# A hybrid conformer / latent-attention / MoE layer: the last reads start one pair earlier, and one-hot and diagonal products add up the last rows

## The reference

```python
for l in range(DEPTH):
    ...
    h = _modulate(xs, g_pre2[l], sh2, sc2)
    xs = xs + gt2 * _rmsnorm(_hier_moe(h, *moe_w), g_post2[l])

def _hier_moe(h, ...):            # 32 experts in 4 groups of 8
    ...                           # one group per token, then the best two experts in it
    e_w = e_top / jnp.sum(e_top, axis=-1, keepdims=True) * g_top
    gates = jnp.sum(jax.nn.one_hot(expert_id, N_EXPERTS) * e_w[..., None], axis=1)
    for e in range(N_EXPERTS):
        he = jax.nn.silu(xt @ w_gate[e]) * (xt @ w_up[e])
        out = out + gates[:, e:e + 1] * (he @ w_down[e])
```

## Time and profile before

| | us |
|---|---|
| median of 3 runs | 673.69 (672.23 to 675.0) |
| the profiled execution | 672.28 |
| its span in the trace | 670.4 |
| PE busy in the span | 575.3 (86%) |
| DVE, ACT, POOL busy | 258.6, 154.7, 54.2 |
| HBM traffic over the span | 269 GB/s |

### The profile page before, as it was taken

The page is one execution under the profiler, slowest core; times in us unless marked ns, Lnnn a source line. Parts: engine busy times, 40 slices in busy tenths (PEclk is TensorE's granted clock), DMA queues, the critical chain, the costliest instruction groups (busy, mean ns, idle before and its releaser), DMA issues.

```text
span 670.4 us, 9777 instructions
## 1 busy us (share of the span) xinstructions
PE 575.3 (86%) x3945; PEld 344.1 (51%) x3945; DVE 258.6 (39%) x470; ACT 154.7 (23%) x318; POOL 54.2 (8%) x77
## 2 busy tenths in 40 slices
PE   0899999999998999999999869988998999777810
PEld 0766665655755455554444756454555555444400
DVE  2414999999533434403333560110101111000017
ACT  3320000012215444422222431111112111111125
POOL 6000000100000000000000010111121121110001
PEclk9999999999899999999999989989999999999965
DMA  9999956000006370009211829999999999999969
GB/s 328 359 385 401 412 199 229 7 8 1 1 1 254 132 294 21 1 9 387 105 64 63 314 58 406 392 407 423 425 421 422 426 423 423 422 425 425 374 246 264
DMA packets 47288, 173.58 MB, mean 259 GB/s; under 512 B 5402, under 2 KB 11899, under 8 KB 34938
## 3 DMA queue, kind: packets, MB, share of 16 engines
q1 hardware_dynamic: 39856, 158.74, 59.2%
q0 software_dynamic: 6096, 12.47, 5.7%
q10 hardware_dynamic: 1274, 1.52, 0.6%
HBM read 162.98 MB, written 17.06 MB: 269 GB/s over the span
## 4 chain that ended last, share of the span: by engine, by line
PE 69%; DMA 14%; SPq 6%; DVE 4%; ACT 3%; issue 3%; ACTq 1%; DVEq 0%; POOLq 0%
PE ps L1496 13%; PE ps L1750 10%; PE ps L1883 10%; PE ps L1899 6%; DMA arena<-in_w_up 6%; SPq L507 5%; DMA arena<-in_w_down 5%; PE ps L1501 4%; PE ps L1497 4%; PE ps L1514 3%; PE ps L1560 3%; PE ps L1709 3%; PE ps L1742 3%; PE ps L1696 2%; DMA x<-in_x_sample 2%
## 5 line engine op out<-in xcount | busy, mean ns | idle before, releaser
L1883 PE MATMUL ps<-arena 128*64 128x256 f32 x992 | 112.4, 384 | 9.6 <-DMA arena<-in_w_gate 4.3
L1496 PE MATMUL ps<-arena 128*128 128x512 f32 x200 | 103.1, 597 | 0.7 <-issue 0.6
L1883 PEld LDWEIGHTS ps<-arena 128*64 128x64 f32 x992 | 72.7, 138 | 52.5 <-issue 13.9
L1150 DVE SCALAR_TENSOR_TENSOR arena<-arena 128x655 f32<-128x655 f32 x116 | 94.8, 897 | 0.4 <-issue 0.2
L1899 PE MATMUL ps<-arena 128*64 128x512 f32 x256 | 60.0, 611 | 16.0 <-ACT arena L992 12.8
L1750 PE MATMUL ps<-arena 128*128 128x512 f32 x160 | 69.7, 594 | 1.9 <-DVE arena L1270 1.0
L1501 PE MATMUL ps<-cst,arena 128*128 128x128 f32 (+2 forms) x349 | 52.0, 297 | 20.0 <-DVE arena L1089 17.0
L1497 PEld LDWEIGHTS ps<-arena 128*128 128x128 f32 x200 | 38.0, 190 | 47.8 <-issue 47.8
L1501 PEld LDWEIGHTS ps<-cst,arena 128*128 128x128 f32 (+2 forms) x349 | 44.6, 180 | 30.3 <-issue 26.9
L1439 DVE TENSOR_TENSOR arena<-arena,ps 128x256 f32<-128x256 f32 x16 | 6.7, 421 | 112.7 <-ACT arena L1021 112.7
L1750 PEld LDWEIGHTS ps<-arena 128*128 128x128 f32 x160 | 30.0, 190 | 38.1 <-issue 37.0
(11 more groups left out here) (272 smaller groups left out, 568.8 us busy)
## 6 DMA issues: line engine op xcount, KB each, us to landing
arena<-in_w_up SPq DMA_DIRECT2D x15, 2048.0 KB, 26.9
arena<-in_w_down SPq DMA_DIRECT2D x15, 2048.0 KB, 20.0
arena<-in_w_gate SPq DMA_DIRECT2D x14, 2048.0 KB, 17.1
arena<-in_w_ada SPq DMA_DIRECT2D x12, 2048.0 KB, 13.5
arena<-y_d SPq DMA_DIRECT2D x10, 512.0 KB, 7.0
arena<-in_w_out SPq DMA_DIRECT2D x1, 4096.0 KB, 13.7
arena<-ada_d SPq DMA_DIRECT2D x8, 512.0 KB, 8.2
x<-in_w_gate SPq DMA_DIRECT2D x2, 2048.0 KB, 27.8
```

Source lines behind the costliest of these rows:

```text
L1150: ins = dve.scalar_tensor_tensor(dst, src, w, dst, ALU.mult, ALU.add)
L1496: mm(pp(name)[:, 0:TS], lhs(k), rhs_s(k), start=k == 0, stop=k == steps - 1)
L1883: last = mm(ps[a:a + ROWS, s, n * FE:(n + 1) * FE], src[:, k, a:a + ROWS], w[:, j, k * FE:(k + 1) * FE], start=k == 0, stop=k == KD - 1)
```

## The change

1. **Zeros first.** Early on, after the first three weight loads, SP writes zeros over the whole of `y_d` (5.2 MB) and waits for that.
2. **The last pair stays in SBUF.** Pair 15 isn't scattered. Its 128 rows are added by a product with `last_hot`, a matrix of 128 rows by 640 tokens with the row's weight in its token's column. DVE makes it from a table of token numbers (`tokens`, a new transfer of 320 KB), the row's token and the row's weight. POOL fetches these weights: it writes `wsel` to HBM after pair 3 and gathers one value per row after pair 5.
3. **Reads earlier.** The ten reads of `y_d` wait for pair 14's scatter and no longer for pair 15; `x_again` is issued behind them.
4. **First shares on PE.** PE multiplies each block's first rows by a diagonal matrix of their weights, in float32 into PSUM, together with the last pair's rows: 4 products of 128x128 by 128x512 a block, and for blocks 3 and 4 two more for the second rows. For blocks 0 to 2 DVE adds the second rows. ACT's scaling goes.
5. **The last norm's vectors.** Instead of two transfers of 512 KB spread over the partitions, SP fetches one partition's row of 2048 values (8 KB). It is issued when pair 13's down product is done, behind the last weight load. PE spreads it by products with a row of ones: `last_gain(0)` ahead of pair 15's gate matmuls, `last_gain(1)` in place of the first `keep_busy`. ACT copies the results out of PSUM.
6. Some semaphores are joined under one name.

The diff, cut to its core:

```diff
+        nothing = W[:, KD * 2 * C + 4096:KD * 2 * C + 4096 + D]
+        tokens = arena[:, 2 * SLOT - 2048:2 * SLOT - 2048 + T]
+        last_hot = arena[:, 2 * SLOT - 2048 + T:2 * SLOT - 2048 + 2 * T]
+        diag0 = arena[:, 2 * SLOT - 2048 + 2 * T:2 * SLOT - 2048 + 3 * T]
...
+        gg2_row = x[0:1, 2:4, :].rearrange("p a b -> p (a b)")
+        last_token, last_weight = stat[:, 2, 0:1], stat[:, 4, 0:1]
+        ON_PE = NT - 2
...
+        LATE_BANK = (0, 2, 6, 4, 0)
+        def summed(b):
+            return ps[:, LATE_BANK[b]:LATE_BANK[b] + 2, :].rearrange("p a b -> p (a b)")
...
             landed(sp, "lnv")
             for n in range(3):
                 load(n)
+            sp.wait_ge(zeroed, 2)
+            sp.dma_start(y_d.rearrange("(n p) d -> p n d", p=P), nothing.unsqueeze(1).broadcast_to([P, 2 * NT, D])).then_inc(y_zero, 16)
+            sp.wait_ge(y_zero, 16)
...
+            sp.wait_ge(e_y, PAIRS - 2)
+            sp.wait_ge(ada_st[5], 32)
+            sp.dma_start(gg2_row, ada_flat[0:2, 5 * D:6 * D]).then_inc(gg2_in, 16)
             sp.wait_ge(e_y, PAIRS - 1)
-            sp.wait_ge(ada_st[5], 32)
-            for v in range(2):
-                sp.dma_start(gg2[:, v, :], bcast(v, 5)).then_inc(gg2_in, 16)
-            for b in range(ADDED, NT):
-                sp.dma_start(x_again[:, b - ADDED, :], out_rows(b)).then_inc(xa_in, 16)
-            for s in range(2):
-                sp.wait_ge(y_st[s], 16 * PAIRS // 2)
+            sp.dma_start(tokens, i["consts"][:, C_ALL:]).then_inc(tables_in, 16)
+            sp.wait_ge(y_st[0], 16 * PAIRS // 2)
+            sp.wait_ge(y_st[1], 16 * (PAIRS // 2 - 1))
             sp.wait_ge(r_pair, PAIRS)
-            sp.wait_ge(e_y, PAIRS)
             for b in range(NT):
                 for c in range(2):
                     sp.dma_start(yg[:, c, b, :], y_d[c * T + b * P:c * T + (b + 1) * P, :]).then_inc(yg_in[b], 16)
+            for b in range(ADDED, NT):
+                sp.dma_start(x_again[:, b - ADDED, :], out_rows(b)).then_inc(xa_in, 16)
             for b in range(ADDED, NT):
                 sp.wait_ge(f_norm, b + 1)
...
+            gp.wait_ge(y_zero, 16)
...
+                if pair == PAIRS - 1:
+                    return
                 gp.wait_ge(e_ys, pair + 1)
-                if pair == PAIRS - 1:
-                    gp.wait_ge(e_ysb, 1)
                 scatter(ys[:, s, :], ids[:, 0, pair:pair + 1], y_st[s])
+                if pair == 3:
+                    gp.wait_ge(wsel_ready, 1)
+                    gp.dma_start(w_d.rearrange("(p n) one -> p (n one)", p=P), wsel[:].rearrange("p c t -> p (c t)")).then_inc(row_weight, 16)
+                if pair == 5:
+                    gp.wait_ge(row_weight, 16)
+                    gp.indirect_dma_start(last_weight, None, w_d, bass.IndirectOffsetOnAxis(idx[:, 2:3], 0),
+                                          bounds_check=P * 2 * NT - 1, oob_is_err=False).then_inc(row_weight, 16)
...
+            def last_gain(v):
+                act.wait_ge(gg2_ps, v + 1)
+                act.activation(gg2[:, v, :], ps[:, 6:8, :].rearrange("p a b -> p (a b)"), ACT.Copy).then_inc(gg2_ready, 1)
...
             def expert_pair(pair, s, last=False, first=False):
                 n = act.value_load(extra[0:1, bass.ds(pair, 1)], min_val=0, max_val=ROUNDS - 1)
+                if last:
+                    last_gain(0)
                 act.wait_ge(e_gu, pair + 1)
                 act.activation(he[:, s, :], ps[:, s, 0:FE], ACT.Silu).then_inc(e_silu, 1)
...
             def norm_sum(b):
-                act.wait_ge(f_mix, b + 1)
-                act.activation(yjunk, yg[:, 1, b, :], ACT.Square, accum_out=stat[:, 3, b:b + 1]).then_inc(f_ss, 1)
+                if b < ON_PE:
+                    act.wait_ge(f_mix, b + 1)
+                else:
+                    act.wait_ge(f_more, b + 1)
+                act.activation(yjunk, yg[:, 1, b, :] if b < ON_PE else summed(b), ACT.Square, accum_out=stat[:, 3, b:b + 1]).then_inc(f_ss, 1)
                 act.wait_ge(f_ss, b + 1)
                 act.activation(stat[:, 5, b:b + 1], stat[:, 3, b:b + 1], ACT.Sqrt, bias=eps, scale=1.0 / D).then_inc(f_sd, 1)
...
             act.activation(stat[0:1, 6, 0:1], stat[0:1, 7, 0:1], ACT.Sqrt)
+            last_gain(1)
             act.wait_ge(e_y, PAIRS)
             act.wait_ge(y_st[1], 16 * (PAIRS // 2 - 1))
             act.activation(ys_last[:, 512:], ps[:, 5, :], ACT.Copy).then_inc(e_ysb, 1)
             for b in range(NT):
-                act.wait_ge(yg_in[b], 32)
-                act.activation(yg[:, 0, b, :], yg[:, 0, b, :], ACT.Copy, scale=wsel[:, 0, b:b + 1]).then_inc(f_first, 1)
-                if b:
-                    norm_sum(b - 1)
-            norm_sum(NT - 1)
+                norm_sum(b)
...
+            row, block = ids[:, 0, PAIRS - 1:PAIRS], idx[:, 3:4]
+            step(dve.tensor_scalar(block, row, P.bit_length() - 1, None, ALU.arith_shift_right))
+            step(dve.tensor_scalar(block, block, -float(P * 2 * NT - 1), None, ALU.mult))
+            dve.scalar_tensor_tensor(idx[:, 2:3], row, float(2 * NT), block, ALU.mult, ALU.add)
+            dve.tensor_copy(last_token, idg[:, 0, PAIRS - 1:PAIRS])
             dve.drain().then_inc(wsel_ready, 1)
...
+                if last:
+                    for b in range(NT):
+                        diag = dve.tensor_scalar(diag0[:, b * P:(b + 1) * P], ident, wsel[:, 0, b:b + 1], None, ALU.mult)
+                    diag.then_inc(hot_ready, 1)
+                    dve.wait_ge(tables_in, 112)
+                    dve.wait_ge(row_weight, 32)
+                    dve.tensor_scalar(last_hot, tokens, last_token, last_weight, ALU.is_equal, ALU.mult).then_inc(hot_ready, 1)
+                    dve.drain()
+                    for b in range(ON_PE, NT):
+                        diag = dve.tensor_scalar(diag1(b), ident, wsel[:, 1, b:b + 1], None, ALU.mult)
+                    diag.then_inc(hot_ready, 1)
...
-            dve.wait_ge(gg2_in, 32)
-            for b in range(NT + 1):
-                if b < NT:
-                    dve.wait_ge(f_first, b + 1)
-                    dve.scalar_tensor_tensor(yg[:, 1, b, :], yg[:, 1, b, :], wsel[:, 1, b:b + 1], yg[:, 0, b, :], ALU.mult, ALU.add)\
-                        .then_inc(f_mix, 1)
-                if b:
-                    n = b - 1
-                    dve.wait_ge(f_sd, n + 1)
-                    dve.reciprocal(stat[:, 5, n:n + 1], stat[:, 5, n:n + 1])
+            def mixed(b):
+                dve.wait_ge(f_more, b + 1)
+                dve.wait_ge(yg_in[b], 32)
+                dve.scalar_tensor_tensor(yg[:, 1, b, :], yg[:, 1, b, :], wsel[:, 1, b:b + 1], summed(b), ALU.mult, ALU.add).then_inc(f_mix, 1)
+            def normalised(b):
+                dve.wait_ge(f_sd, b + 1)
+                dve.reciprocal(stat[:, 5, b:b + 1], stat[:, 5, b:b + 1])
+                dve.drain()
+                src = yg[:, 1, b, :] if b < ON_PE else summed(b)
+                last = dve.scalar_tensor_tensor(yo[:, b, :], src, stat[:, 5, b:b + 1], gg2[:, min(b, 1), :], ALU.mult, ALU.mult)
+                if b >= ADDED:
                     dve.drain()
-                    last = dve.scalar_tensor_tensor(yo[:, n, :], yg[:, 1, n, :], stat[:, 5, n:n + 1], gg2[:, min(n, 1), :], ALU.mult, ALU.mult)
-                    if n >= ADDED:
-                        dve.drain()
-                        dve.wait_ge(xa_in, 16 * (NT - ADDED))
-                        last = dve.tensor_tensor(yo[:, n, :], yo[:, n, :], x_again[:, n - ADDED, :], ALU.add)
-                    last.then_inc(f_norm, 1)
+                    dve.wait_ge(xa_in, 16 * (NT - ADDED))
+                    last = dve.tensor_tensor(yo[:, b, :], yo[:, b, :], x_again[:, b - ADDED, :], ALU.add)
+                last.then_inc(f_norm, 1)
+            mixed(0)
+            dve.wait_ge(gg2_ready, 2)
+            for b in range(1, ON_PE):
+                mixed(b)
+                normalised(b - 1)
+            for b in range(ON_PE - 1, NT):
+                normalised(b)
...
+            def last_gain(v):
+                for half in range(2):
+                    at = v * D + half * 512
+                    one = mm(ps[:, 6 + half, :], ones[0:1, :], gg2_row[:, at:at + 512], start=True, stop=True)
+                one.then_inc(gg2_ps, 1)
...
+                if last:
+                    pe.wait_ge(gg2_in, 16)
+                    last_gain(0)
                 gate_up(s, first, xT[:, s], e_gate, e_gu, pair == 0)
                 if pair == 0:
...
+                if last:
+                    pe.wait_ge(gg2_ready, 1)
                 with pe.If(n > 0):
...
                 if last:
-                    keep_busy(3, 7)
+                    last_gain(1)
                 pe.wait_ge(e_h, pair + 1)
                 hidden_to_columns(s, he[:, s, :], e_ht)
                 if last:
-                    keep_busy(3, 7)
+                    keep_busy(3, 0)
                 pe.wait_ge(e_hT, pair + 1)
...
```

(63 more changed lines are left out.)

9 lines of the change are left out of this document (3 added, 6 removed).

## The result

The changed kernel is slower: 680.88 us median of 20 runs (676.37 to 686.66) against 674.92 of the kernel before (20 runs, 671.91 to 679.46), ratio 1.008 with a 95% interval of 1.0063 to 1.0098. The forecast was 672.9 in a range of 664 to 678, so the time lies outside the range, and it moved the other way than the likeliest case.

What follows compares the result with a forecast made beforehand. Weight loads set the experts' pace, then a serial tail. Row landing at 631.5, plus 16.2 to the down product's end, 14.3 for products and 7.7 finish: 669.7 against 670.4, so -0.7, 672.9 us; range 664 to 678.

Steps and rivals of the forecast that it cites:

- the likeliest case: Whole kernel: PE waits for the 8 KB row, and the time changes by -0.7 us to 672.9; chance 0.5.
- 24, at 0.597 = 14.3: PE's sums after the last down product: 24 products of 128x512 at 0.597 us each, 14.3 us.
- The saving in the tail: Stretch behind the last down product: shrinks from 31.3 to 22.0 us, a saving of 9.3.
- The row's queue: SP's DMA queue before pair 15: the 8 KB row waits behind the last weights, and PE waits for it until 631.5.
- G: Time the 8 KB row lands and PE can start on it: 631.5, the middle of 627.8 and 635.3.
- the slowest engine carries a part: Rival on the row's transfer: it lands at 635.3, making the kernel 3.1 to 4.1 us slower; chance 0.23.
- The terms behind the row: From the row's landing to pair 15's down product's end: `last_gain(0)`, gate and up, `last_gain(1)`, down product; 16.2 us.
- Gate and up: Pair 15's gate and up matmuls on PE after the row's wait: 8.7 us, with the clock lowered after the pause.
- The chances: Likeliest case 0.5, no wait for the row 0.2, slowest engine 0.23, reads late or something else 0.07.
- The covers: Early reads (9 us of cover), zeros, DVE's matrices and ACT's copies: hidden behind other work, taken to cost nothing.
- the finish behind the last product: Block 4, from its complete sum to the span's end: 7.7 us.

Runs made afterwards that it cites:

- the two kernels that repeat this stretch: Changed kernel with 20 products in the tail instead of 24, ratio 1.0071; changed kernel with the 8 KB row as two transfers, ratio 1.0087.

## Why the prediction was wrong

**The step that failed** is the term "24, at 0.597 = 14.3". A float32 product of 128x512 leaves two records in the trace, which overlap: each lasts 0.597 us, but in a long run a product takes 0.86 to 0.87. The "x200" of the earlier trace rows counts records, and the kernel there has half as many products. The stream took 20.87 us, 6.5 more than the sum had. The rows ahead of the prediction held the sign: each call of `keep_busy` makes three products and stands in the earlier trace rows as x6. The 64 and 16 matmuls that the description of the kernel before gives for a pair are such counts too; the code issues 32 and 8.

With that term alone set right the sum would have stood at +5.9 us instead of -0.7, where the ratio says +5.4. That it comes so near is partly luck, since two other errors nearly cancel (below). The saving in the tail, forecast as 9.3 us, was 3.0 (31.2 to 28.2). The one-hot half of the stream (10 products, 8.7 us) costs nearly what the scatter and the reads behind it had cost, 9.4.

**The row's queue** was right as a mechanism; the length of the wait wasn't. G was forecast as 631.5 in a trace in which pair 14's down product ended at 623.8, so a wait of 7.7 us. The row landed at 611.06 + 19.45 = 630.5, but everything ran 1.7 us later there, and PE waited 5.2 us, and 4.3 and 4.5 in the two kernels that repeat this stretch: 2.5 to 3.4 us less than forecast. Taking the middle of the engines' finishing times was a guess; the row's two engines were among the early ones. The queue explains the wait (it is gone on another queue), and the wait explains the loss against the kernel before (8 us come back without it, more than the 5.4 lost, and 6.6 us more of it cost about 7.5 us). What it doesn't explain is the distance from the forecast, which had a longer wait in it. The Trainium skill's rule on the share of the engines (DMA: Bandwidth & Descriptors, section Why a DMA increments its semaphore by 16 and not by 1), that only the engines which carry a transfer count, agrees with the trace: two landings for this row, sixteen for the one that was cut. The rival "the slowest engine carries a part" became true only then. Its wait was as forecast (635.3 - 623.8 = 11.5, measured 11.8). Its step above the main case, 7.5 us where 3.8 had been forecast, was larger mainly because the main case's own wait was shorter.

**The terms behind the row** were too small together: from PE's start on the row to the down product's end 18.7 to 21.8 us (in the four kernels that wait for it) where 16.2 had been forecast. In the changed kernel's trace, the 21.8, `last_gain(0)` took 3.75 instead of 1.2: the same miscount (0.87 a product) at half the clock; at full clock it is 1.98. Gate and up took 9.8 instead of 8.7 (8.5 to 9.5 in the other three). From there to the down product 3.3 instead of 2.6, since `last_gain(1)` has the miscount as well. The down product took 4.9 instead of 3.7, at the lower clock, which no step had foreseen and which is absent in the other three. The wait came out too long by 2.5 and these terms too short by 5.6, so that the last pair took 26.9 us where 23.9 had been forecast; in the two that repeat it, 23.0 and 23.5, the errors cancel. In this trace the misses of last pair and tail, 3.0 and 6.2 us, and the later end of pair 14 (1.7) make up the whole distance from 669.7 to 680.6.

**The chances** were misplaced for a reason of their own. The sum stood 0.7 us below zero with every unknown rounded the kind way: the slowed ones products were kept for the range's end, and DVE's and ACT's times on PSUM were waved through. The bound on a product's price, from one group's mean, had no second row beside it; the time between starts in the chain would have been that row.

**The covers held.** The reads were issued 1.8 us later than forecast and were never waited for in the changed kernel; the zeros cost nothing that the times tell, although the load behind them was issued 3.4 us later; DVE's matrices took 2.1 us in their gap; ACT's copies were in time; the finish behind the last product took 7.4 us where 7.7 was forecast.

## What to carry to other kernels

Take the price of an instruction from the distance between starts in a long run of it, and the number from the code; a group's mean and count can count one product twice and let it overlap itself. Before a compute engine is made to wait for a small transfer, ask what stands ahead of it in its queue: 8 KB behind weights took 19 us, and the same 8 KB on another queue took 4.9. Count how many engines carry it, too: cut over sixteen instead of two, the same 8 KB took 28. When work that was a round trip through memory becomes work on an engine, price it at that engine's real pace first: here it gave 3 us of an expected 9. A quarter of the new products could go back to engines that had gaps: together with the vectors behind the reads that made the fastest version, though no run shows what the products' share of it is in the times. One trace of a kernel isn't its typical case: the last pair took 26.9 us in one and 23.0 in another for the same work.

## What the runs showed of the hardware

- A small transfer behind large ones on the same queue waits for the engines that carry it, not for the large transfer's end: PE waited 4.3 to 5.2 us when the row was 2 runs of 4 KB, and 11.8 when it was cut along a dimension of 16. The semaphore records show two landings for the one and sixteen, spread over 9.5 us, for the other. The Trainium skill, DMA: Bandwidth & Descriptors, section Why a DMA increments its semaphore by 16 and not by 1, says that the slowest dimension of both sides decides how many engines take part; the waits and the landings agree. Dimensions that are contiguous on both sides were joined again in one kernel, and nothing changed.
- PE's granted clock fell to 0.50 with PE busy (632 to 634 in the kernel with 20 idle products, 648 to 650 in the changed one), and the last pair's down product then took 4.9 to 5.35 us instead of 3.65. It took that long in four of the seven traces with one-row ones products ahead of it and in none of the six with other products or none. In the pairs 1 to 14 ahead of it, where there are no such products, 7 of 182 took 5.2 to 5.35, one of them in the kernel before (pair 1, 5.21 behind 1.97 us of idle time), so the one-row products can't be the only cause; what the cause is stays open.
- Idle products of 128x128 at full clock: 0.23 us each (36 in 8.30), two records each.
